# Scaled quarter corrections, earlier row transfers, and angle steps shared out around the fourth quarter, in a two-layer block on one core

## The reference, cut to what matters

```python
cos, sin = rope_tables(positions)          # angles = positions * inv, 8 per row
cond = silu(c)                             # one vector of 1024
mod = cond @ ada_w[l] + ada_b[l]           # shift sh1, scale sc1, ... 1024 each
h = rmsnorm(x, norm1_g[l]) * (1 + sc1) + sh1
proj = h @ w_in[l] + b_in[l]
```

## Time and profile before

| what | us |
|---|---|
| median of three runs | 1454.11 (1453.11 to 1454.91) |
| profiled execution | 1455.57 |
| its span on the chip | 1453.8 |
| PE busy in the span | 1424.6 (98%) |
| POOL busy in the span | 1209.7 (83%) |
| ACT busy, DVE busy | 758.7, 718.3 |
| PE busy in the first 50 us | 34.54 |
| PE busy from 50 to 120 us | 68.69 |

### The profile page before, as it was taken

How to read it: one execution, slowest core, us unless ns; L and a number is a source line. 1 busy time by engine, 2 the same in 40 slices (tenths; PEclk the granted TensorE clock), 3 DMA queues, 4 the chain that set the end, 5 groups by cost and what they waited for, 6 DMA issues and landing times.

```text
span 1453.8 us, 21473 instructions
## 1 busy us (share of the span) xinstructions
PE 1424.6 (98%) x7560; PEld 1193.2 (82%) x7560; DVE 718.3 (49%) x1555; ACT 758.7 (52%) x1279; POOL 1209.7 (83%) x984
## 2 busy tenths in 40 slices
PE   6999999999999999999999999999999999999997
PEld 4798777799988987778888888878888888788886
DVE  6863654766643754754566303454650044655202
ACT  4435775644444335765654445574654345655442
POOL 3799989898878987559898997967999977789995
PEclk9999999999999999999999999999999999999999
DMA  9994546678875986337675565644555656345561
GB/s 364 401 352 160 198 166 228 237 296 317 311 256 164 401 310 222 109 101 232 215 247 205 188 203 162 200 143 137 195 190 194 222 164 188 131 164 199 193 200 56
DMA packets 147651, 313.35 MB, mean 216 GB/s; under 512 B 11076, under 2 KB 31960, under 8 KB 147544
## 3 DMA queue, kind: packets, MB, share of 16 engines
q1 hardware_dynamic: 145504, 310.55, 62.2%
q10 hardware_dynamic: 2040, 1.42, 0.3%
HBM read 310.87 MB, written 1.06 MB: 215 GB/s over the span
## 4 chain that ended last, share of the span: by engine, by line
PE 86%; POOL 4%; DVE 4%; DMA 2%; ACT 2%; issue 1%; SPq 0%; POOLq 0%; DVEq 0%; ACTq 0%
PE bank L810 54%; PE bank L855 12%; PE bank L856 8%; POOL lo_units L747 4%; PE bank L853 3%; DMA raw_units<-in_w_ffn_out 1%; PE bank L1018 1%; ACT hi_units L1359 1%; PE bank L1002 1%; DMA raw_units<-in_w_ffn_tiles 1%; PE bank L988 1%; PE bank L891 1%; PE bank L1105 1%; PE bank L1034 1%; PE bank L1070 1%
## 5 line engine op out<-in xcount | busy, mean ns | idle before, releaser
L747 POOL TENSOR_TENSOR lo_units<-raw_units,hi_units 128x512 fp32r<-128x512 f32 (+3 forms) x928 | 1150.5, 1275 | 223.3 <-ACT hi_units L1359 222.1
L1359 ACT ACTIVATE hi_units<-raw_units 128x1024 fp32r<-128x1024 f32 (+1 forms) x470 | 482.8, 1030 | 404.7 <-PE bank L810 235.6
L810 PE MATMUL bank<-hi_units,turned 128*128 128x512 f32 (+3 forms) x1600 | 442.2, 391 | 5.9 <-DVE turned L1888 4.3
L810 PEld LDWEIGHTS bank<-hi_units,turned 128*128 128x128 f32 x1600 | 291.7, 189 | 57.7 <-DVE turned L1888 6.3
L856 PE MATMUL bank<-turned,lo_units 128*128 128x256 f32 x1024 | 288.1, 281 | 0.0
L810 PE MATMUL bank<-hi_units,turned_wide 128*128 128x512 f32 x992 | 274.6, 391 | 0.0
L855 PE MATMUL bank<-turned,hi_units 128*128 128x512 f32 x736 | 260.1, 398 | 0.0
L810 PE MATMUL bank<-lo_units,turned 128*128 128x512 f32 (+3 forms) x800 | 253.1, 383 | 0.8 <-POOL lo_units L747 0.5
L810 PEld LDWEIGHTS bank<-hi_units,turned_wide 128*128 128x128 f32 x992 | 185.3, 188 | 38.5 <-issue 0.5
L856 PEld LDWEIGHTS bank<-turned,lo_units 128*128 128x128 f32 x1024 | 194.2, 190 | 0.2
L810 PEld LDWEIGHTS bank<-lo_units,turned 128*128 128x128 f32 x800 | 150.0, 188 | 30.9 <-POOL lo_units L747 3.6
(11 more groups left out here) (256 smaller groups left out, 1288.1 us busy)
## 6 DMA issues: line engine op xcount, KB each, us to landing
ada_units<-in_ada_w SPq DMA_DIRECT2D x72, 512.0 KB, 7.2
raw_units<-in_w_ffn_tiles SPq DMA_DIRECT2D x72, 512.0 KB, 4.7
raw_units<-in_mlp_w_out SPq DMA_DIRECT2D x64, 512.0 KB, 3.2
raw_units<-in_mlp_w_tiles SPq DMA_DIRECT2D x56, 512.0 KB, 3.2
raw_units<-in_w_in SPq DMA_DIRECT2D x56, 458.0 KB, 9.9
raw_units<-in_w_in SPq DMA_DIRECT2D x48, 512.0 KB, 6.8
raw_units<-in_w_ffn_out SPq DMA_DIRECT2D x44, 512.0 KB, 3.8
raw_units<-in_moba_w_qkv SPq DMA_DIRECT2D x24, 512.0 KB, 3.7
```

The lines of the kernel that those rows point to most:

```text
L747: pool.tensor_tensor(LO[:, s, b, 0:w], RAW[:, u["slot"], b, 0:w], HI_[:, s, b, 0:w].bitcast(F32), ALU.subtract).then_inc(lo_ready.sem, lo_ ...
L810: ins = pe.matmul(BANK[2 * c["pair"] + t][:, 0:w], (A[a] if A is BT else A[:, a])[:, part, t * P:(t + 1) * P], W[:, s, b, 0:w], start=(i = ...
L1359: act.activation(HI_[:, s, 0:n, 0:w], RAW[:, u["slot"], 0:n, 0:w], ACT.Copy)\
```

## The change

The four column sums of a quarter are multiplied by a row of gains and ones and then have a constant added, both instructions with one operand in PSUM; (1 + bias) * gain is made once, ahead of the quarters, in `first_constants`. ACT reads factor and shift from one place. SP issues the rows `x` one transfer earlier, ahead of i = 2. PE's two `keep_running` pairs both stand behind the first column sums. On DVE, `tables` and the first three steps of the angles (now `turns`) stand ahead of the fourth quarter's `first_columns`; the nine steps that are left stay where they were. On ACT, three more unit copies (units 8, 9 and 10) stand ahead of the sine.

```diff
-    FIRST_BIAS, FIRST_GAIN = NM[:, 0:2 * KT], NM[:, 2 * KT:3 * KT]
-    BIASED, GAINED = RS[:, 0:2 * KT], MX[:, 0:KT]
+    FIRST_BIAS, FIRST_GAIN, FIRST_SCALED = NM[:, 0:2 * KT], NM[:, 2 * KT:4 * KT], RS[:, 0:2 * KT]
...
-                if (l, c, i) == (0, 0, 3):
+                if (l, c, i) == (0, 0, 2):
                     for t in range(NT):
                         sp.dma_start(X[:, t, :], dram["x"][0, t * P:(t + 1) * P, :]).then_inc(x_in[t], 16)
...
-                keep_running(1, BANK[3])
                 column_sums(0)
-                keep_running(1, BANK[3])
+                keep_running(2, BANK[3])
...
-                ins = act.activation(part, part, ACT.Identity, scale=GAINED[:, 2 * q + k:2 * q + k + 1], bias=BIASED[:, 4 * q + 2 + k:4 * q + 3 + k])
+                ins = act.activation(part, part, ACT.Identity, scale=FIRST_SCALED[:, 4 * q + k:4 * q + k + 1],
+                                     bias=FIRST_SCALED[:, 4 * q + 2 + k:4 * q + 3 + k])
...
-        act.dma_start(NM[:, 0:3 * KT], dram["first_columns"]).then_inc(first_in, 16)
+        act.dma_start(NM[:, 0:4 * KT], dram["first_columns"]).then_inc(first_in, 16)
...
                     prep(2 * q + 2)
+                prep(2 * N_FIRST + 3)
                 for what, dst in (("sin", SIN), ("cos", COS)):
...
         def first_columns(q):
 
-            dve.wait_ge(first_in, 16)
             dve.wait_ge(product.sem, product.at(("columns", q)))
             cols = slice(4 * q, 4 * q + 4)
-            link(v.tensor_tensor(BIASED[:, cols], BANK[SB_[1]][:, cols], FIRST_BIAS[:, cols], ALU.add))
-            say(v.scalar_tensor_tensor(GAINED[:, 2 * q:2 * q + 2], BIASED[:, 4 * q:4 * q + 2], 1.0, FIRST_GAIN[:, 2 * q:2 * q + 2], ALU.add, ALU.mult),
-                ("columns", q))
+            sums = BANK[SB_[1]][:, cols]
+            link(v.tensor_tensor(sums, sums, FIRST_GAIN[:, cols], ALU.mult))
+            say(v.tensor_tensor(FIRST_SCALED[:, cols], sums, FIRST_BIAS[:, cols], ALU.add), ("columns", q))
+
+        def first_constants():
+
+            dve.wait_ge(first_in, 16)
+            scales = lambda a: a.rearrange("p (q four) -> p q four", q=N_FIRST)[:, :, 0:2]
+            link(v.scalar_tensor_tensor(scales(FIRST_BIAS), scales(FIRST_BIAS), 1.0, scales(FIRST_GAIN), ALU.add, ALU.mult))
...
-        def angles():
+        def turns():
...
                 link(v.tensor_scalar(ANG[:, 8 * t:8 * t + 8], con("inv"), POSF[:, t:t + 1], None, ALU.mult))
+
+        def angles():
...
         say(v.reciprocal(RR[:, 0:NT], RSTD), "inverse root")
+        first_constants()
...
                         first_sum(q + 1, 0)
+                    else:
+                        tables()
+                        turns()
                     first_columns(q)
...
-                tables()
                 angles()
```

More of the change, by code:

```diff
@@ L2593, in in_quarters @@
     first = np.stack([w[:, c].reshape(P, KT, CW) for c in cols])
-    columns = np.concatenate([b[c].reshape(4, P) for c in cols] + [g.reshape(KT, P)]).T
+    ones = np.ones((2, P), g.dtype)
+    gains = [np.concatenate([g.reshape(N_FIRST, 2, P)[q], ones]) for q in range(N_FIRST)]
+    columns = np.concatenate([b[c].reshape(4, P) for c in cols] + gains).T
     return {"in_ada_first": np.ascontiguousarray(first), "in_first_columns": np.ascontiguousarray(columns)}
```

## The result

| kernel | median us | runs | span of the profiled execution |
|---|---|---|---|
| before | 1454.24 (1453.11 to 1454.91) | 6 | 1453.8 |
| changed | 1459.18 (1457.39 to 1460.61) | 6 | 1458.8 |

The change makes the kernel slower: ratio 1.0035, 95% interval 1.0023 to 1.0047, 4.9 us. The opening accounts for it: PE is done with chunks 2 and 3 at 53.27 + 19.43 = 72.70 before and at 54.74 + 22.77 = 77.51 after, 4.81 later, and the spans of the two profiles differ by 5.0.

What follows compares the result with a forecast made beforehand. The opening was taken to bound the kernel, since PE hardly waits afterwards. Chunk 2's start, 55.40, plus 1.37 for the clock, less 52.43, made 4.34 us longer: median 1458.4, range 1455.0 to 1460.2.

Steps and rivals of the forecast that it cites:

- Rows x: Opening: x issued one transfer earlier, but DVE's slices 2 to 5 stand ahead of the reciprocal; gain none to 0.1 us.
- `first_hi(0)`: ACT, quarter 0: moves from 18.70 to 17.39, held behind the copy of unit 0; 1.31 us gained.
- The first unit at full clock: PE's first unit begins at 19.86, ahead of the clock's fall, in place of 21.17 and 3.90 us long.
- 8.0 us for a quarter: Quarters 1 to 3: DVE's eight slices set the pace, 8.01 us each.
- `tables` and `turns`: DVE ahead of the fourth column step: first step waits for POOL, column step about 0.77 us late; bounds 0 and 0.77.
- The nine angle steps: DVE after quarter 3: first escapes, eight each end with a POOL subtraction, 9.40 us; `angles` ends at 54.14, not 50.53.
- Chunk 2 on PE: PE waits 5.5 us for the drain of chunk 0 and begins chunk 2 at 55.40.
- Clock: PE's granted clock falls after the wait ahead of chunk 2, costing 1.37 us; bounds 0 and 1.7.

Runs made afterwards that it cites:

- steps in PSUM: Changed kernel with intermediate results of the nine angle steps kept in PSUM, same copies and POOL work; median 1450.61 us, 2.87 less than before.
- rows x later: Changed kernel with the rows x issued one transfer later again, as before the change; 1456.51 us in one run.
- copies alone: Kernel before with nothing changed but the three unit copies ahead of the sine; median 1460.24 us, 6.76 more than before.
- one copy: Changed kernel with one unit copy (unit 8) ahead of the sine in place of three; median 1452.83 us, 1.12 less than before.
- no copies: Changed kernel without the three unit copies ahead of the sine; median 1451.73 us, 1.75 less than before.
- tables in the pause: Changed kernel with angle steps in PSUM, plus `tables` and `turns` moved behind the fourth column step; median 1450.97 us, 2.98 less than before.

## Why the prediction was right

The forecast was 1458.4, by one term after the other 4.34 us more; measured are 4.81 in the profile and 4.94 between the medians. The way in which the loss comes about was the one forecast; four sizes in the sum were off, and their errors partly cancel.

- Rows x: nothing gained, as forecast, and the profile shows why (ACT waits 1.70 for the reciprocal behind slices 4 and 5).
- `first_hi(0)`: forecast 17.39, measured 16.74. The weights of unit 0 were there at 15.65 and not at 16.38, so its copy was over at 16.62, and what `first_hi(0)` followed was DVE's column step, which ended at 16.71: not the copy, as forecast. The landing lies between 15.35 and 16.45 in the ten profiles, with x at either place, so this size could not have been known better.
- The first unit at full clock, then 8.0 us for a quarter (24.72 to 32.71 on ACT): as forecast.
- `tables` and `turns`: mis-sized. 1.1 and not 0.77: the column step comes 2.38 after DVE's slices end at 39.08, where it was 1.25. Unit 6 was copied late, POOL had a pause in between, and two steps met a subtraction and not one. In the two profiles where POOL ran its four subtractions in a row there (steps in PSUM, rows x later), it comes 2.03 and 2.04 after, 0.8 lost, as forecast.
- The nine angle steps: eight held up, first one escaped, as forecast; 9.0 us and not 9.40.
- Chunk 2 on PE: 54.74, forecast 55.40. The 0.65 of quarter 0 and the 0.4 of the angle steps, less the 0.3 of `tables`, are the difference.
- Clock: mis-sized, 2.5 and not 1.37, and above the bound of 1.7. I took the loss after the wait ahead of 21.17, where the clock was back some 3 us after PE had begun:

```profile
24.00:25.00 1.00, 1.00 (x6) 0.98 1.03 415
```

Here it stayed low until past 60, over 5 us of work. The bound held only if the low stretch was as long as that one. It need not be, even after nearly the same wait: in the profile of the copies alone PE waited 2.84 ahead of 20.58, and the clock stood at 0.50 until past 26. What sets the length is open, so one profile could not size this term.

That the sum came out within 0.5 is in part luck: the 0.65 and the 0.4 of the angle steps went against the 1.1 of the clock and the 0.3 of `tables`.

## What to carry to other kernels

Before more work is given to POOL earlier, look at what small DVE steps with all operands in SBUF will then run beside it, and at what waits behind them: each of the kinds met here (`tensor_scalar`, `scalar_tensor_tensor`, a cast) costs the rest of a POOL instruction, 1.1 us for a step of 0.18, however little it computes. Not every kind does: the 32 reciprocals of 128x2 at line 2016 of the kernel before, all in SBUF, took 165 to 169 ns each, in a kernel where POOL is at work for 83% of the span. Giving such a step one operand or its result in PSUM took the cost away; moving the steps behind the drain only moved the wait to whoever needed their result next. A wait on PE can have a second price in the clock after it, here half as much again (2.5 on top of 5.1); after 1.54, with one copy, there was none.

## What the runs showed of the hardware that was not expected

The granted clock fell to 0.50 for some 3.4 us shortly after 40 us in four of ten profiled executions (no copies, steps in PSUM, copies alone, tables in the pause), after a wait of PE of no more than 1.2 us ahead of the column sums; in the others, with the same instructions on PE up to there, it stayed at 1.00. What decides this is open.

Landing of the first weight unit differs by 1.1 us between profiles, and the time behind the opening by 4 us. Both are more than most terms of the sum here.
